# Stationary operands read with a step of two: rounded part and remainder of a weight alternate in one buffer

## The reference

```python
for l in range(DEPTH):
    h = rms_norm_2(x, norm_mix_pre[l])
    proj = h @ w_in[l]                      # 1024 -> 12 slices of 256
    ...
    mix = jnp.concatenate([y_conf, y_sb, y_ret, y_sc], axis=-1) @ w_out[l]
    x = x + rms_norm_2(mix, norm_mix_post[l])
    f = conv_ffn(rms_norm_2(x, norm_ffn_pre[l]), ffn_up[l], ffn_conv_w[l], ffn_down[l])
    x = x + rms_norm_2(f, norm_ffn_post[l])
```

## Time and profile before

| | |
|---|---|
| median of 3 runs | 2684.9 us (2681.97 to 2691.93) |
| profiled execution, its own time | 2690.91 us |
| its span | 2689.1 us |
| mean granted TensorE clock | 0.974 |
| first block, with its experts | to about 1463 us |
| second block, layer 0 (in, mixers, out, up, down) | 1463 to 2093 us |
| second block, layer 1 | 2093 to 2689 us |

### The profile page before, as it was taken

One profiled execution on the slowest core, in us unless ns is written; L12 is line 12 of the kernel. 1 busy time (PEld: TensorE's weight loads), 2 busy tenths in 40 slices (PEclk: granted clock), 3 DMA queues, 4 the chain that ended last, 5 costly groups with the idle time before them and its releaser, 6 DMA issues.

```text
span 2689.1 us, 36859 instructions
## 1 busy us (share of the span) xinstructions
PE 2505.2 (93%) x14582; PEld 1853.1 (69%) x14582; DVE 1077.2 (40%) x1628; ACT 754.3 (28%) x1221; POOL 181.6 (7%) x302
## 2 busy tenths in 40 slices
PE   8997999888899979998888999999999999999999
PEld 7675666544576656665454777888888877888887
DVE  4753011100445541110001666655543666555542
ACT  3530000000245410000001353443332454433431
POOL 0001111111000001111111010000000010000000
PEclk9997999999999989999999999999999999999999
DMA  5339999999622189999998312223232212222231
GB/s 174 84 144 368 414 414 416 419 414 411 257 94 79 40 342 411 411 412 415 417 419 340 139 63 86 83 91 101 94 126 94 102 56 99 81 93 95 94 125 55
DMA packets 175401, 576.56 MB, mean 214 GB/s; under 512 B 20560, under 2 KB 104080, under 8 KB 125618
## 3 DMA queue, kind: packets, MB, share of 16 engines
q1 hardware_dynamic: 164722, 558.07, 53.8%
q0 software_dynamic: 10560, 16.81, 1.8%
HBM read 569.56 MB, written 23.07 MB: 220 GB/s over the span
## 4 chain that ended last, share of the span: by engine, by line
PE 62%; SPq 19%; DMA 3%; DVE 3%; issue 3%; ACT 2%; DVEq 0%; POOLq 0%; ACTq 0%
PE ps L240 14%; PE ps L242 14%; PE ps L241 14%; SPq L1183 13%; SPq L1189 6%; PE ps L1333 6%; PE ps L1351 4%; DMA first_weights<-in_moe_w_up 2%; PE ps L1303 1%; ACT lat_probs L1841 1%; PE ps L1650 1%; PE ps L2340 1%; PE ps L1666 1%; PE ps L2376 1%; DMA open_rows<-r_y 1%
## 5 line engine op out<-in xcount | busy, mean ns | idle before, releaser
L240 PE MATMUL ps<-l_h_hi,l_w_hi 128*128 128x512 f32 x896 | 352.9, 394 | 0.0
L241 PE MATMUL ps<-l_h_lo,l_w_hi 128*128 128x512 f32 x896 | 348.8, 389 | 0.0
L242 PE MATMUL ps<-l_h_hi,l_w_lo 128*128 128x512 f32 x896 | 348.7, 389 | 0.0
L1333 PE MATMUL ps<-first_weights,moe_xsT 128*64 128x256 f32 x2688 | 309.5, 380 | 39.6 <-DMA first_weights<-in_moe_w_up 26.9
L1412 DVE TENSOR_TENSOR moe_hid<-moe_silu,ps 128x256 f32<-128x256 f32 x64 | 27.0, 421 | 767.9 <-PE ps L1333 767.9
L1333 PEld LDWEIGHTS ps<-first_weights,moe_xsT 128*64 128x64 f32 x2688 | 225.8, 137 | 132.9 <-issue 82.7
L2892 DVE TENSOR_TENSOR l_w_lo<-l_raw,l_w_hi 128x2048 fp32r<-128x2048 f32 x76 | 174.0, 2292 | 270.1 <-ACT l_w_hi L2637 269.9
L1385 ACT ACTIVATE moe_ys<-ps 128x512 f32<-128x512 f32 x64 | 38.2, 597 | 672.3 <-PE ps L1351 672.3
L1351 PE MATMUL ps<-first_weights,moe_hidT 128*64 128x512 f32 x672 | 177.2, 675 | 38.3 <-DVE moe_hidT L1414 38.3
L2637 ACT ACTIVATE l_w_hi<-l_raw 128x2048 fp32r<-128x2048 f32 x76 | 145.2, 1914 | 179.8 <-PE ps L242 168.9
L240 PEld LDWEIGHTS ps<-l_h_hi,l_w_hi 128*128 128x128 f32 x896 | 168.2, 188 | 37.5 <-issue 2.9
(11 more groups left out here) (589 smaller groups left out, 4304.2 us busy)
## 6 DMA issues: line engine op xcount, KB each, us to landing
first_weights<-in_moe_w_up SPq DMA_DIRECT2D x84, 1024.0 KB, 27.9
first_weights<-in_moe_w_down SPq DMA_DIRECT2D x84, 1024.0 KB, 27.7
first_weights<-in_moe_w_gate SPq DMA_DIRECT2D x84, 1024.0 KB, 27.4
first_ring<-in_moe_w_up SPq DMA_DIRECT2D x44, 1024.0 KB, 27.5
first_ring<-in_moe_w_down SPq DMA_DIRECT2D x44, 1024.0 KB, 27.6
l_raw<-in_ffn_up SPq DMA_DIRECT2D x44, 1024.0 KB, 5.0
first_ring<-in_moe_w_gate SPq DMA_DIRECT2D x40, 1024.0 KB, 27.6
l_raw<-in_w_in SPq DMA_DIRECT2D x22, 1024.0 KB, 4.9
```

Source lines behind the costliest of these rows:

```text
L240: pe.matmul(out, stationary[0], moving[0], start=first, stop=False)
L241: pe.matmul(out, stationary[0], moving[1], start=False, stop=False)
L242: return pe.matmul(out, stationary[1], moving[0], start=False, stop=last)
L1333: ins = pe.matmul(k.ps[64 * h:64 * h + 64, 2 + m, 0:256], xsT[:, j, :], piece[:, j % 4, 256 * h:256 * h + 256], start=j == 0, stop=j == ND ...
```

## The change

Each pair of high and low part becomes one buffer of twice the size. `alternating` reads such a buffer as two operands, whose elements alternate: the high part is elements 0, 2, 4, ..., the low part 1, 3, 5, ... `halves` reads it as first half and second half, as before. A buffer that is used as stationary operand is alternating, one that moves is in halves; the slots of `w` serve both, by the number of the piece. Changed so are `first` of both openings, `w`, `outs`, `second_up`, `last_down`, `act`, `y_sb` and `y_ret`. h, y_conf and y_sc, and all operands of the window and the latent layer but the latent layer's two first pieces, stay as they were.

```diff
+def alternating(y):
+    return tuple(y.rearrange("p (c x) -> p c x", x=2)[:, :, n] for n in range(2))
+
+def halves(y):
+    n = y.shape[-1] // 2
+    return y[:, 0:n], y[:, n:]
...
-        self.split = [plan.split(f"first{n}", hi, lo, [P, 2048]) for n, (hi, lo) in enumerate(split_kb)]
+        self.split = [alternating(plan.put(f"first{n}", kb, [P, 2 * 2048], F32R)[:, :]) for n, kb in enumerate(split_kb)]
...
-    h, w = Split(st, "h", [P, ND, SEQ]), Split(st, "w", [P, 2, 2048])
+    h, w = Split(st, "h", [P, ND, SEQ]), [st.sb(f"w{n}", [P, 2 * 2048], F32R) for n in range(2)]
...
-    y_sb, y_ret = plan.put("y_sb", 52.25, [P, 2, 2, SEQ], F32R), plan.put("y_ret", 60.25, [P, 2, 2, SEQ], F32R)
+    y_sb, y_ret = ([alternating(y[:, i, :]) for i in range(2)] for y in (plan.put("y_sb", 52.25, [P, 2, 2 * SEQ], F32R), plan.put("y_ret", 60.25, [P, 2, 2 * SEQ], F32R)))
...
-    outs = [plan.split(f"outs{n}", 8 * n, 16 + 8 * n, [P, 2048]) for n in range(2)]
-    second_up = plan.split("second_up", 76.3125, 84.3125, [P, 2048])
-    last_down = plan.split("last_down", 0, 44, [P, 2048])
-    act_t = plan.split("act", 0, 44, [P, FF_TILES, SEQ])
+    outs = [plan.put(f"outs{n}", 16 * n, [P, 2 * 2048], F32R) for n in range(2)]
+    second_up = plan.put("second_up", 76.3125, [P, 2 * 2048], F32R)
+    last_down = plan.put("last_down", 32, [P, 2 * 2048], F32R)
+    acts = plan.put("act", 0, [P, FF_TILES, 2 * SEQ], F32R)
+    act_t = [[alternating(acts[:, f, :])[n] for f in range(FF_TILES)] for n in range(2)]
...
-    in_w = [(w.hi[:, n, :], w.lo[:, n, :]) for n in range(2)]
+    in_w = lambda n: (halves if n in moving_pieces else alternating)(w[n % 2][:, :])
+    moving_pieces = (SBV, RV, AT_OUT + 2, AT_OUT + 3, *range(AT_DOWN, PIECES))
...
-    ring += [tuple(y[:, :] for y in x) for x in outs] + in_w
-    ring += [ring[AT_OUT], tuple(y[:, :] for y in second_up)] + [in_w[n % 2] for n in range(2, 2 * STEPS)]
-    ring += [(in_w + in_h)[d % 4] for d in range(STEPS - 1)] + [tuple(y[:, :] for y in last_down)]
+    ring += [halves(y[:, :]) for y in outs] + [in_w(AT_OUT + n) for n in range(2, OUT_CHUNKS)]
+    ring += [alternating(y[:, :]) for y in (outs[0], second_up)] + [in_w(n) for n in range(AT_UP + 2, AT_DOWN)]
+    ring += [in_h[d % 2] if d % 4 >= 2 else in_w(AT_DOWN + d) for d in range(STEPS - 1)] + [halves(last_down[:, :])]
...
                     else:
-                        act.wait_ge(x.down_used, 2)
+                        act.wait_ge(x.down_used, 6)
```

More of the change, by code:

```diff
@@ L2132, in second_block @@
     y_conf, y_sc = plan.split("y_conf", 48, 44, [P, 2, SEQ]), plan.split("y_sc", 72.25, 68.25, [P, 2, SEQ])
-    y_sb, y_ret = plan.put("y_sb", 52.25, [P, 2, 2, SEQ], F32R), plan.put("y_ret", 60.25, [P, 2, 2, SEQ], F32R)
-    y_of = lambda f: {0: [x[:, f % 2, :] for x in y_conf], 1: [y_sb[:, f % 2, n, :] for n in range(2)],
-                      2: [y_ret[:, f % 2, n, :] for n in range(2)], 3: [x[:, f % 2, :] for x in y_sc]}[f // 2]
+    y_sb, y_ret = ([alternating(y[:, i, :]) for i in range(2)] for y in (plan.put("y_sb", 52.25, [P, 2, 2 * SEQ], F32R), plan.put("y_ret", 60.25, [P, 2, 2 * SEQ], F32R)))
+    y_of = lambda f: {0: [x[:, f % 2, :] for x in y_conf], 1: y_sb[f % 2], 2: y_ret[f % 2], 3: [x[:, f % 2, :] for x in y_sc]}[f // 2]
     assert plan.at == cl.plan.at
     first = cl.split
-    outs = [plan.split(f"outs{n}", 8 * n, 16 + 8 * n, [P, 2048]) for n in range(2)]
-    second_up = plan.split("second_up", 76.3125, 84.3125, [P, 2048])
-    last_down = plan.split("last_down", 0, 44, [P, 2048])
-    act_t = plan.split("act", 0, 44, [P, FF_TILES, SEQ])
+    outs = [plan.put(f"outs{n}", 16 * n, [P, 2 * 2048], F32R) for n in range(2)]
[3 more added lines that the diff above has]
+    act_t = [[alternating(acts[:, f, :])[n] for f in range(FF_TILES)] for n in range(2)]
     conv = plan.put("conv", 90.5, [P, 4, SEQ])
@@ L2145, in second_block @@
     out_gains = [plan.put(f"out_gain{n}", 36 + 4 * n, [P, D]) for n in range(2)]
-    end_gains = [plan.put(f"end_gain{n}", 24 + 4 * n, [P, D]) for n in range(2)]
+    end_gains = [plan.put(f"end_gain{n}", 48 + 4 * n, [P, D]) for n in range(2)]
     out_xn = [plan.put("out_xn0", 32, [P, D]), plan.put("out_xn1", 92.3125, [P, D])]
@@ L2149, in second_block @@
     squares = end_gains[1]
-    rows = plan.put("rows", 32, [P, DEPTH, 3, P])
-    cm = AfterMix(st, plan, "c", 0, 84)
+    rows = plan.put("rows", 44, [P, DEPTH, 3, P])
+    cm = AfterMix(st, plan, "c", 32, 88)
     cl.lend(st, cm)
-    in_w = [(w.hi[:, n, :], w.lo[:, n, :]) for n in range(2)]
+    in_w = lambda n: (halves if n in moving_pieces else alternating)(w[n % 2][:, :])
+    moving_pieces = (SBV, RV, AT_OUT + 2, AT_OUT + 3, *range(AT_DOWN, PIECES))
     in_h = [tuple(y[:, 4 * n:4 * n + 4, :].rearrange("p a s -> p (a s)") for y in (h.hi, h.lo)) for n in range(2)]
-    ring = [tuple(y[:, :] for y in x) for x in first] + [in_w[n % 2] for n in range(2, N_SLICES)]
-    ring += [tuple(y[:, :] for y in x) for x in outs] + in_w
-    ring += [ring[AT_OUT], tuple(y[:, :] for y in second_up)] + [in_w[n % 2] for n in range(2, 2 * STEPS)]
-    ring += [(in_w + in_h)[d % 4] for d in range(STEPS - 1)] + [tuple(y[:, :] for y in last_down)]
+    ring = list(first) + [in_w(n) for n in range(2, N_SLICES)]
+    ring += [halves(y[:, :]) for y in outs] + [in_w(AT_OUT + n) for n in range(2, OUT_CHUNKS)]
+    ring += [alternating(y[:, :]) for y in (outs[0], second_up)] + [in_w(n) for n in range(AT_UP + 2, AT_DOWN)]
+    ring += [in_h[d % 2] if d % 4 >= 2 else in_w(AT_DOWN + d) for d in range(STEPS - 1)] + [halves(last_down[:, :])]
     views = lambda n, j: [x.rearrange("p (j c) -> p j c", j=j) for x in ring[n]]
@@ L2544, in down @@
                             f = 2 * d + j
-                            ins = split_matmul(pe, k.ps[:, 2 * t + half, :], [tile_cols(y, t)[:, f, :] for y in act_t],
+                            ins = split_matmul(pe, k.ps[:, 2 * t + half, :], [y[f][:, t * P:(t + 1) * P] for y in act_t],
                                                [y[:, j, half * 512:(half + 1) * 512] for y in (whi, wlo)], f == 0, f == FF_TILES - 1)
@@ L2723, in high_of_sb @@
                     act.wait_ge(x.sb_mixed, i + 1)
-                    act.activation(y_sb[:, i, 0, :], k.ps[:, 6, :], ACT.Copy).then_inc(x.y_high, 1)
+                    act.activation(y_sb[i][0], k.ps[:, 6, :], ACT.Copy).then_inc(x.y_high, 1)
                 def keep_ret(i):
@@ L2816, in mixer @@
                     act.wait_ge(x.y_made, i + 3)
-                    act.activation(y_ret[:, i, 0, :], ro[:, i, :], ACT.Copy).then_inc(x.y_high, 1)
+                    act.activation(y_ret[i][0], ro[:, i, :], ACT.Copy).then_inc(x.y_high, 1)
                 keep(27, scb[:, 1, :])
@@ L2841, in feed_forward @@
                         act.wait_ge(x.product, 2 * i + m + 1)
-                        act.activation(act_t[0][:, 2 * i + m, :], conv_of(m), ACT.Copy).then_inc(x.act_hi, 1)
+                        act.activation(act_t[0][2 * i + m], conv_of(m), ACT.Copy).then_inc(x.act_hi, 1)
                 for d in range(2, STEPS):
@@ L3014, in mixer @@
                 taps(6)
-                low_of_y(0, y_sb[:, 0, 1, :], k.ps[:, 6, :], y_sb[:, 0, 0, :])
+                low_of_y(0, y_sb[0][1], k.ps[:, 6, :], y_sb[0][0])
                 rope(1)
@@ L3029, in mixer @@
                 decayed(0, 1)
-                low_of_y(1, y_sb[:, 1, 1, :], k.ps[:, 6, :], y_sb[:, 1, 0, :])
+                low_of_y(1, y_sb[1][1], k.ps[:, 6, :], y_sb[1][0])
                 decayed(0, 2)
@@ L3067, in mixer @@
                 for i in range(2):
-                    low_of_y(4 + i, y_ret[:, i, 1, :], ro[:, i, :], y_ret[:, i, 0, :])
+                    low_of_y(4 + i, y_ret[i][1], ro[:, i, :], y_ret[i][0])
                 for i in range(2):
@@ L3093, in feed_forward @@
                         dve.wait_ge(x.act_hi, 2 * i + m + 1)
[L3094 removed]
+                        dve.tensor_tensor(act_t[1][2 * i + m], conv_of(m), act_t[0][2 * i + m].bitcast(F32), ALU.subtract).then_inc(x.act_lo, 1)
                 for d in range(2, STEPS):
@@ L3158, in program @@
     weights = ExpertWeights(k, first)
-    openings = [Collect(k, Plan(k, "open0", base), routes[0], 0, (112, 120, 128, 136), 96, 170, ((32, 40), (48, 56))),
-                Collect(k, Plan(k, "open1", base + SECOND_AT), routes[1], 1, (36, 44, 68, 76), 24, 0, ((8, 52), (16, 60)))]
+    openings = [Collect(k, Plan(k, "open0", base), routes[0], 0, (112, 120, 128, 136), 96, 170, (32, 48)),
+                Collect(k, Plan(k, "open1", base + SECOND_AT), routes[1], 1, (56, 64, 72, 80), 40, 32, (0, 16))]
     def held_first(sp):
```

## The result

| | before | after |
|---|---|---|
| median, 4 runs each on one chip | 2687.41 us (2681.97 to 2691.93) | 2714.78 us (2709.45 to 2716.44) |
| profiled execution, its own time | 2690.91 us | 2715.33 us |
| its span, mean granted clock | 2689.1 us, 0.974 | 2713.5 us, 0.976 |

The ratio is 1.0099, with a 95% interval of 1.0074 to 1.0125: the change costs some 27 us (20 to 34 us by the interval). The medians and ratios further down are of executions like these; one of the eleven with everything in halves took 4590.5 us at a granted clock of 0.82, and its ratio leaves it out.

What follows compares the result with a forecast made beforehand. TensorE was taken to bound the kernel nearly everywhere from 1490 us on. Gains of 43 us (512 columns) and 5 us (256 columns), less 1 us not returned, made 47 us: 2638 us, range 2627 to 2700 us.

Steps and rivals of the forecast that it cites:

- Steps 1 and 2: Converted stationary operands: 3936 matmuls of 512 columns and 960 of 256 affected, bounded between 54 us gained and 97 us lost.
- The worst bound: Stationary loads at half rate: hidden behind 512 columns, but 256-column matmuls go from 120 to at least 221 ns, 97 us more.
- Step 3: Stationary and moving streams at one speed meet once: 512-column matmuls 227 to 216 ns, 43 us saved; 256-column ones 5 us.
- The excess grows: Rival, chance 0.17: a load spanning twice the bytes costs another 13.3 ns on each of 4896 matmuls, 65 us, 2750 us.
- No difference: Rival, chance 0.15: the 13.3 ns per matmul are a fixed cost of a four-byte load, whatever its addresses; 2685 us.
- The load becomes the limit: Rival, chance 0.08: the slower load limits 256-column matmuls, 97 us more less up to 43 us, 2739 to 2782 us.
- Step 4: Weight conversions on ScalarE and VectorE: no cost from writing with a step; if they doubled, 8 us in the mixers.
- Step 5: Mixers, where TensorE waits for conversions and taps: 0.5 us of its gain not returned per layer, 1 us.
- Step 6: Moved buffers: only ScalarE's wait before the last down piece changes, costing nothing.

Runs made afterwards that it cites:

- matmuls alone: Kernels without the reference's computation, timing groups of 96 matmuls over steps, places and widths: 512 columns 226.7 ns at stationary step 1, 233.3 ns at step 2.
- act_alone: The changed kernel with all pairs in halves except act, which alone alternates: 2694.98 us against 2686.62 us for the kernel before, ratio 1.0029.

## Why the prediction was wrong

**Steps 1 and 2, the counts and bounds.** The count of 3936 and 960 matmuls was right, and so was where to look: the loss is a few ns on each of 3936 matmuls and next to nothing else. The worst bound, a load at half its rate, doesn't occur with a step of 2 (193 against 188 ns). The Trainium skill ("SBUF — State Buffer", Specifications (TRN2), Cachelines) asks for two hits per 16-byte line for full bandwidth; the load nearly agrees (two hits 193 ns against 188 with four; a step of 4, so one hit, 310 ns).

**Step 3 failed**, by mechanism and sign. It read the 13.3 ns as the load's and the moving operand's streams meeting, and concluded that streams of one speed meet only once: "227 going to 216 ns". They went to 233. The one observation under it was sound, that addresses matter (second_up's 118 ns against 120), but it was one row, with 256 columns, and I took a sign from it for 512. The matmuls alone show that the same shift of 64 bytes saves 2.2 ns with 256 columns and costs 6.7 ns with 512. The layout before was already the fastest of all that were tried with float32r at 512 columns: 544 cycles with step 1 and both operands equally placed; everything else gives 549 or more. The other thing I took for evidence was that plain float32 pays only 2.2 ns over; but bfloat16, which takes one pass like float32r, also stands at 216 ns, so the pass count doesn't explain it. Bfloat16's elements have half the bytes, so whether the bytes that the moving operand reads per cycle matter stays open.

**The rivals.** "The excess grows" had the sign and the deciding point right ("as soon as the 512-column distance is above 227"), at 6.7 ns in place of 13.3, and of the kernel's two widths only at 512 columns, so 27 us and not 65; its mechanism, a cycle lost for each piece of memory passed, is refuted by the step of 0 and by 64 and 32 stationary columns. "No difference" failed at 512 columns; at 256 it held for the step itself (120 ns with either), and only second_up, which lay 64 bytes on, lost 2 ns. "The load becomes the limit" holds at a step of 4, where 256 columns go to 233 ns; a step of 3 was not run at that width.

**Step 4, the conversions,** was nearly right: nothing on VectorE, but not nothing on ScalarE, where a piece of w goes from 1914 ns to 2058 in the up projection and to 2.09 to 2.15 us elsewhere. That was hidden where I had said: no new wait of TensorE came in. **Step 5** had no gain to lose. **Step 6** was right: with everything in halves the ratio is 0.9997.

What stays open is why 512 columns fall into 544 cycles in one case and 560 in the other. The engine is loading for 8.45 of 10.20 us in place, and for 8.46 of 10.50 us with the shift of 64 bytes, so the length of the load doesn't set the distance. That it depends on the relative place of the two operands, comes and goes with the width (5.3 ns at 496 columns, none at 504, 6.7 at 512), and gets no better with a shorter load, looks like a rhythm that two streams settle into. That is a guess: no run here shows the thing they share.

## What to carry to other kernels

Where a kernel is bound by back-to-back matmuls, its distance from start to start is a property of layout that a page of busy times doesn't show: take 90 distances from a window, and measure the new layout in a kernel of matmuls alone before rebuilding any buffers. With the distances of such a kernel both full-kernel costs came out within 1 us of the medians (26.7 us against 27.4 for the change, 19.2 against 19.0 for w shifted), though the first median is itself known only to some 7 us, and act_alone came out at 8.4 us where they gave 7.0. By these runs, give both operands of float32r matmuls of 512 columns a step of 1 and the same place on the 256-byte grid (226.7 ns; every other float32r case had 228.9 or more); if a step can't be avoided, put it where 256 columns move. And a mechanism read from one row may have another sign in the shape that makes up the time.

## What the runs showed of the hardware

- float32r, 128 x 128 stationary: 512 columns 226.7 ns with operands equally placed and 233.3 with a stationary step of 2 or a shift of 64 bytes; 256 columns 120 ns, or 117.8 with the shift. A shift acts by the relative place of the two operands, modulo 256 bytes. Bfloat16 has 216 ns, as the Trainium skill's "TensorE: Matmul & The Clock Gate" (Back-to-back issue gap) gives by its formula for 512 columns; no float32r group here reached that.
- A moving float32r operand with a step of 2 takes 451 ns, twice as long, although it still has two hits per 16-byte line; there the rule of the Trainium skill ("SBUF — State Buffer", Specifications (TRN2), Cachelines) doesn't hold. The change kept all moving operands in halves.
- 504 and 512 columns take the same 226.7 ns at best, and 504 columns keep it with a step of 2.
- The load of a stationary operand takes 188 ns with a step of 1, 193 with 2, 253 with 3, 310 with 4.
- ScalarE takes some 8% longer to write 2048 float32r elements with a step of 2 (w in the up projection 2058 ns in place of 1914, second_up 2090 where it took 1924 with everything in halves); VectorE takes 2293 ns in place of 2292, no longer.
